# An encoder layer on one core: the first head's scores, one part of a filter and the first bias table change places

## What is computed

```python
xn = rmsnorm(h, norm_g)
z = xn @ w_in                       # 2048 x 16384
hy_in, hy_gate, fn_in, fn_gate, qkv, na_gate, merge = split(z)
u, x1, x2 = split(short_conv(hy_in, conv_w, conv_b))
kf = hyena_filters(...)             # a small MLP, an envelope, an FFT
y_a = (x2 * fftconv(x1 * fftconv(u, kf[0]), kf[1])) * silu(hy_gate)
y_b = fourier_mixer(fn_in) * silu(fn_gate)
y_c = neighborhood_attention(q, k, v, rpb, meta_bias) * silu(na_gate)
g_a, g_b, g_c = sigmoid(merge)
m = g_a * (y_a @ w_a) + g_b * (y_b @ w_b) + g_c * (y_c @ w_c)
out = rmsnorm(h + m @ w_out, final_g)[16:]
```

## Time and profile before

| | |
|---|---|
| median of the runs | 1156.02 us |
| the profiled execution's own time | 1155.4 us |
| its span, first to last instruction | 1153.6 us |
| granted TensorE clock, mean over the span | 0.997 |
| TensorE (PE) busy | 1120.5 us, 97% |
| weight loads (PEld) busy | 1013.8 us, 88% |
| VectorE (DVE) busy | 765.9 us, 66% |
| ScalarE (ACT) busy | 560.9 us, 49% |
| GpSimd (POOL) busy | 59.5 us, 5% |
| share of TensorE in the chain that ended last | 84% |
| share of VectorE in it | 9% |

### The profile page before, as it was taken

The page is one execution under the profiler, slowest core; times in us unless marked ns, Lnnn a source line. Parts: engine busy times, 40 slices in busy tenths (PEclk is TensorE's granted clock), DMA queues, the critical chain, the costliest instruction groups (busy, mean ns, idle before and its releaser), DMA issues.

```text
span 1153.6 us, 17302 instructions
## 1 busy us (share of the span) xinstructions
PE 1120.5 (97%) x7222; PEld 1013.8 (88%) x7222; DVE 765.9 (66%) x1141; ACT 560.9 (49%) x771; POOL 59.5 (5%) x98
## 2 busy tenths in 40 slices
PE   5999999999999999999999999999999999999997
PEld 3898999999999999999999988888888888888886
DVE  6767788668788587886887865554554455455554
ACT  6545645555555455554465464444444443444443
POOL 4011000300000300002000000000000000000000
PEclk9999999999999999999999999999999999999999
DMA  8635333553435533435544375555555555556652
GB/s 307 232 122 178 132 125 131 179 207 113 147 119 170 190 128 134 147 129 174 183 146 142 124 264 190 198 189 189 182 188 187 199 193 182 182 189 243 260 184 110
DMA packets 30494, 201.56 MB, mean 175 GB/s; under 512 B 3872, under 2 KB 4192, under 8 KB 7744
## 3 DMA queue, kind: packets, MB, share of 16 engines
q1 hardware_dynamic: 25024, 180.16, 44.7%
q0 software_dynamic: 5248, 19.77, 5.0%
q10 hardware_dynamic: 144, 0.52, 0.1%
HBM read 195.19 MB, written 5.24 MB: 174 GB/s over the span
## 4 chain that ended last, share of the span: by engine, by line
PE 84%; DVE 9%; issue 3%; ACT 3%; DMA 0%; ACTq 0%; DVEq 0%
PE ps L563 26%; PE ps L565 26%; PE ps L564 26%; DVE w_lo L1298 2%; ACT w_hi L978 1%; PE ps L568 1%; DVE k_lo L1298 1%; PE ps L587 1%; DVE sd L1390 1%; DVE hm L1385 1%; PE ps L717 1%; DVE q_two L1496 1%; DVE u L1484 0%; PE ps L677 0%; DVE prod L1533 0%
## 5 line engine op out<-in xcount | busy, mean ns | idle before, releaser
L1298 DVE TENSOR_TENSOR w_lo<-raw,w_hi 128x1024 fp32r<-128x1024 f32 x336 | 407.6, 1224 | 281.4 <-ACT w_hi L978 280.1
L978 ACT ACTIVATE w_hi<-raw 128x1024 fp32r<-128x1024 f32 x336 | 351.1, 1057 | 373.7 <-PE ps L565 372.9
L563 PE MATMUL ps<-xn_hi,w_hi 128*128 128x272 f32 (+2 forms) x1280 | 367.7, 287 | 0.0
L565 PE MATMUL ps<-xn_hi,w_lo 128*128 128x272 f32 (+2 forms) x1280 | 365.6, 286 | 0.0
L564 PE MATMUL ps<-xn_lo,w_hi 128*128 128x272 f32 (+2 forms) x1280 | 365.6, 286 | 0.0
L563 PEld LDWEIGHTS ps<-xn_hi,w_hi 128*128 128x128 f32 x1280 | 242.5, 189 | 2.1
L564 PEld LDWEIGHTS ps<-xn_lo,w_hi 128*128 128x128 f32 x1280 | 242.1, 189 | 0.8
L565 PEld LDWEIGHTS ps<-xn_hi,w_lo 128*128 128x128 f32 x1280 | 242.2, 189 | 0.0
L563 PE MATMUL ps<-w_hi,xn_hi 128*128 128x512 f32 x384 | 152.3, 397 | 0.0
L565 PE MATMUL ps<-w_hi,xn_lo 128*128 128x512 f32 x384 | 150.9, 393 | 0.0
L564 PE MATMUL ps<-w_lo,xn_hi 128*128 128x512 f32 x384 | 150.6, 392 | 0.0
(11 more groups left out here) (245 smaller groups left out, 1355.7 us busy)
## 6 DMA issues: line engine op xcount, KB each, us to landing
raw<-w_stream SPq DMA_DIRECT2D x168, 1024.0 KB, 4.9
branch_y<-ystage POOLq DMA_DIRECT2D x12, 256.0 KB, 3.2
y_raw<-branch_y POOLq DMA_DIRECT2D x3, 1024.0 KB, 7.1
xin<-x SPq DMA_DIRECT2D x2, 1024.0 KB, 7.1
w4s<-w POOLq DMA_DIRECT2D x16, 128.0 KB, 4.5
absd<-decay POOLq DMA_DIRECT2D x8, 256.0 KB, 6.5
h<-x POOLq DMA_DIRECT2D x2, 1024.0 KB, 9.4
rows_t<-rpb POOLq DMA_DIRECT2D x8, 219.0 KB, 6.2
```

What stands on the lines that cost most here:

```text
L563: mm(out_ap, a_hi, b_hi, start=first, stop=False)
L565: return mm(out_ap, a_lo, b_hi, start=False, stop=last)
L978: A(w_hi[:, w % 2, part, :], raw[:, w % 4, 1024 * part:1024 * part + 1024], ACT.Copy).then_inc(hi_done, 1)
L1298: return V.tensor_tensor(dst, src, hi.bitcast(F32), ALU.subtract)
```

## The change

Three things move. No arithmetic is added or removed.

1. TensorE issues `scores(0)` behind slab 7 instead of slab 6, and VectorE and ScalarE treat head 0 like the other heads: `biased(c, 0)` at the head of VectorE's step 7, ahead of the split of slab 9, `normalized(c, 0)` behind that split, `soft(c, 0)` behind ScalarE's split of slab 9. Before, all three stood at the end of step 6.
2. The third part of filter group 2c + 1: `sum_and_difference` moves from between the halves of slab 5's split (step 3) to ahead of both; `sd_high` and `sd_low` from behind both halves to between them.
3. POOL's `make_bias(0)` moves ahead of the store of `ystage`, and waits for `kx_mm`, which TensorE's `filter_x(0)` (the even bins of group 0) raises before the chunks begin.

```diff
             load_filter(1)
+            pool.wait_ge(kx_mm, 1)
+            make_bias(0)
             store_y(0, 1, yb_done)
-            make_bias(0)
...
-                    if t == 6:
+                    if t == 7:
                         pe.wait_ge(proj_read, blocks_read(c, "k"))
                         pe.wait_ge(k_done, 2 * c + 2)
                         pe.wait_ge(kf_evac, 2 * c + 2)
                         scores(0)
...
-                    if at_ == (3, 2):
+                    if at_ == (3, 1):
                         sd_high(a, 2)
...
-                    if t == 6:
-                        soft(c, 0)
...
-                    if t in (9, 11, 13):
+                    if t in (7, 9, 11, 13):
                         soft(c, (t - 7) // 2)
...
                     if at_ == (3, 0):
                         sd_low(a, 1)
+                        sum_and_difference(a, 2)
                     if at_ == (3, 1):
-                        sum_and_difference(a, 2)
-                    if at_ == (3, 2):
                         sd_low(a, 2)
...
-                    if t in (9, 11, 13):
+                    if t in (7, 9, 11, 13):
                         biased(c, (t - 7) // 2)
                     split(slab_of(c, t) + 2, 0)
...
-                    if t in (9, 11, 13):
+                    if t in (7, 9, 11, 13):
                         normalized(c, (t - 7) // 2)
...
-                    if t == 6:
-                        biased(c, 0)
-                        normalized(c, 0)
```

## The result

The changed kernel takes **1148.06 us**, the median of its runs, beside 1156.12 us for the kernel before. The medians lie 8.06 us apart; the ratio is 0.9925, with a 95% interval of 0.9908 to 0.9942, so about 0.7% faster. The forecast was 8.6 us and 1147.4. One of the five executions of the changed kernel was slow, with 2247.13 us; the ratio goes without it, and nothing here shows its cause. The profiled execution of the changed kernel took 1148.06 us, its span is 1146.2 us.

The account below looks back on a forecast made before the run. TensorE's stops bound the kernel: 4.5 us saved in chunk 0 plus 4.1 in chunks 1 to 3, 8.6 off the profiled 1155.4, gives 1146.8; 0.6 added for the median gives 1147.4, range 1145.0 to 1150.8.

Parts of the forecast that it names:

- What bounds the kernel: TensorE, busy 97% of the span: time can come only from its stops, 11.6 us in all apart from the start-up.
- entry and 0.27: Each TensorE wait costs its listed entry plus 0.27 us, read from the stop before the scores in chunk 1.
- The bias: Chunk 0: moving `make_bias(0)` sooner removes the 1.8 us stop on `folded`; its new place costs TensorE 0.
- The two ways in which I let it go: New place: VectorE's two `w_lo` keep POOL off, or POOL gets in and the second slips some 3.7 us.
- The rule I weighed: Shared port lock held for one instruction; the prediction instead read VectorE's `sd` as blocked for four POOL additions, 0.91 us each.
- The third part: Filter waits on `sd_rest` go, 0.60 us in chunks 1 to 3, 1.0 in chunk 0; VectorE's queue runs 0.5 us sooner.
- The scores: The 1.76 us stop on `k_lo` goes; chunks 1 to 3 get a 1.0 us wait on slab 8's `w_lo`, chunk 0 none.
- The sum: Whole kernel: 4.5 us in chunk 0 plus 4.1 in chunks 1 to 3, 8.6 off, giving 1147.4 us.
- A: Rival, all chunks: every stop goes, 11.6 us, giving 1144.4; chance 0.12.
- B: Rival at slab 8: the wait moves and keeps its 1.5 us in all four chunks, giving 1150.4; chance 0.2.
- C: Rival in chunk 0: VectorE's loss isn't the bias, so `folded`'s 1.8 us stays and slab 8's wait comes; 1150.2; chance 0.07.
- D: Rival, slower: head 0's softmax has one slab, so `turn_p` stops TensorE every chunk; 1158.6 needs a chain about 8.9 us; chance 0.03.

Follow-up runs that it names:

- the two probes: Two kernels: the changed kernel with POOL's bias additions of chunks 1 to 3 timed to meet VectorE work; each ran once, only timelines read, no ratio.
- the second probe: Changed kernel, POOL's additions started by u's evacuation: chunk 1 directly, 2 behind a DMA issue, 3 behind two clears; `sd` 3.97 us in chunk 2, 1.09 in 3; no ratio.

## Why the prediction was right

**What bounds the kernel.** Right: TensorE's stops were the whole matter. They came to 11.6 us before by the rule "entry and 0.27", less 3 x 1.05 left after gives 8.45; the stretch says 8.44. (The stop that is left costs its entry of 0.81 and 0.24.)

**The bias.** That the old place cost chunk 0 the wait on `folded` and VectorE's lead: right, 3.26 us come back with it. That the new place costs TensorE nothing: right. The two ways in which I let it go were both wrong, though: neither did VectorE's pair keep POOL off nor did the second `w_lo` slip by 3.7 us; they took turns, and it lost 0.75.

**The rule I weighed.** Here a step failed. I read from the 3.85 us that VectorE is held for four additions, set that above the page, and took it as what could happen at the new place. At the new place, and in five of six meetings in the two probes, an operation of VectorE waited for one addition at most, as the Trainium skill says (SBUF — State Buffer, "SBUF: two separate sides": the lock is held for one instruction). The row was true, but of a condition of its own, by the probes the DMA issue in front, which that section does not name. It did not reach the sum, since the cover was long enough for either.

**The third part.** 0.60 in each of chunks 1 to 3 and 1.0 in chunk 0 went, the lead is 0.52 for 0.54, the half slab's split stayed hidden, and `forward(0)` followed with the 0.3 us of room I gave it (`uT` whole at 253.57, wanted at 253.87).

**The scores.** The new wait was forecast at 0.9, 1.0 with the restart; it is 1.09 between two starts where 0.125 is normal, 1.05 in cost. None in chunk 0: right, with 0.5 us to spare. The softmax does not reach `turn_p`, and the exponential has ended when VectorE comes to scale.

**The sum.** 8.6 forecast, 8.44 in the stretch, 8.06 between the medians. The spans of the two profiled executions differ by 7.4 only, since the changed kernel entered the stretch 0.99 us later; 0.94 of that is already there at the first filter matmul of all (37.14 and 38.08), ahead of anything that the change moves. The forecast took the start-up as fixed, and added 0.6 us because one median lay that far above one execution; no row stands behind that term. That the median came within 0.7 us of 1147.4 is partly luck: the same kernel's median was 1149.75 when it ran again.

**The rivals.** A needed no wait at slab 8 and shows what was left: 3.15 us, which moving the third product then took. B (the wait keeps its size) is refuted by 0.81 instead of about 1.4. C is refuted by the old place's kernel, and D, the slower case, by the absence of any wait on `sco`: the chain from the first bias addition to the end of the scaling takes 4.0 us with the two `w_lo` inside it (278.88 to 282.89), against the 6.07 of a slab.

## What to carry to other kernels

When a wait is removed from an engine that is nearly always busy, the next wait is found by asking when each later operand is ready and when it will now be wanted: both numbers can be read from the trace before, and here they gave the new wait to 0.1 us. As long as a later wait on the same engine remains, moving work sooner on it is worth the lead that it gains there (2.23 us for 4 x 0.54), not the wait that it removes (2.8 us). And where a single row contradicts a rule, look at what stands in front of it before taking the row for the rule.

## What was not expected

- POOL and VectorE took turns, one instruction each, at the bias' new place and in five of the six meetings in the probes, with losses of 0.2 to 0.8 us for each operation of VectorE; an operation was held for a whole row of four additions, 3.84 to 3.97 us, only where POOL had issued a DMA just before them and the operation began within 0.1 us of the first.
- TensorE's wait at `filter_x(0)` had two lengths, 1.2 and 2.6 us, in different executions, and the longer one was no delay: `filter_x(0)` started 23.1 us behind the first filter matmul either way. In all seven profiles with the longer one the granted clock was 1.00 early and 0.50 from 62 to 66 us, and the start-up took 2.5 us more from that matmul to the stretch. Of the others two (the scores undone, the second probe) had 0.61 and 0.65 from 62 to 66 us and took 1.5 us more, the rest 1.00. So where the low clock falls alone moves the time of a kernel by more than some of the parts tried here; what sets it, no run here shows.
